# Two edits to a two-layer encoder kernel: the forgetting product over 128 rows, and the last down projection with positions on partitions

## The reference, cut to what matters

```python
def forgetting_attention(q, k, v, log_f):
    F = jnp.cumsum(log_f, axis=1)
    ...
        logits = jnp.einsum('bqhd,bshd->bhqs', q_blk, k) * (d ** -0.5)
        logits = logits + Fq[..., None] - Fk[:, :, None, :]
        logits = jnp.where(key_pos[None, :] <= qpos[:, None], logits, -jnp.inf)
    ...
    for l in range(DEPTH):
        h = h + hybrid_mixer(rmsnorm(h, norm1_g[l]), ...)
        h = h + (jax.nn.silu(gate) * up) @ w_down[l]     # gate, up: causal conv of h @ w_up
    return h * rsqrt(mean(h * h) + 1e-6) * final_g
```

## Time and profile before

| | before |
|---|---|
| median of 3 runs | 1531.95 us (1531.93 to 1532.08) |
| profiled execution | 1532.42 us |
| span of the profile | 1530.6 us |
| mean granted TensorE clock | 0.995 |
| TensorE (PE) busy | 1505.0 us, 98% of the span, 7184 products |
| VectorE (DVE) busy | 1015.4 us, 66% |
| ScalarE (ACT) busy | 705.4 us, 46% |
| GpSimd (POOL) busy | 49.3 us, 3% |
| HBM read, written | 136.13 MB, 2.10 MB |

### The profile page before, as it was taken

One profiled execution on the slowest core, in us unless ns is written; L12 is line 12 of the kernel. 1 busy time (PEld: TensorE's weight loads), 2 busy tenths in 40 slices (PEclk: granted clock), 3 DMA queues, 4 the chain that ended last, 5 costly groups with the idle time before them and its releaser, 6 DMA issues.

```text
span 1530.6 us, 20233 instructions
## 1 busy us (share of the span) xinstructions
PE 1505.0 (98%) x7184; PEld 1234.0 (81%) x7184; DVE 1015.4 (66%) x1818; ACT 705.4 (46%) x1214; POOL 49.3 (3%) x39
## 2 busy tenths in 40 slices
PE   7899999999999999999999999999999999999998
PEld 5688887788888888888878888778888888888886
DVE  5788775555587743777468887655557776257754
ACT  5766654433444422443376666433344443134444
POOL 0000000000200000000110000000020000000011
PEclk9999999999999999999999999999999999999998
DMA  6221212223232233232432222122323222332232
GB/s 228 69 75 64 77 55 80 73 84 117 84 109 93 86 94 113 96 96 69 126 123 83 70 70 70 56 82 70 110 69 124 97 96 83 97 109 96 84 91 73
DMA packets 43861, 139.27 MB, mean 91 GB/s; under 512 B 5508, under 2 KB 5636, under 8 KB 43528
## 3 DMA queue, kind: packets, MB, share of 16 engines
q1 hardware_dynamic: 43344, 137.45, 28.1%
q10 hardware_dynamic: 440, 0.80, 0.2%
HBM read 136.13 MB, written 2.10 MB: 90 GB/s over the span
## 4 chain that ended last, share of the span: by engine, by line
PE 92%; DVE 3%; ACT 2%; issue 1%; DMA 1%; SPq 0%; ACTq 0%; DVEq 0%
PE dense L574 28%; PE dense L576 28%; PE dense L575 28%; PE turned L619 2%; PE branch L633 2%; PE scores L605 1%; PE scores L606 1%; PE scores L609 1%; ACT tmp L927 1%; DMA h<-in_x 1%; DVE act L1154 0%; ACT whi L799 0%; PE dense L785 0%; DVE wlo L1074 0%; DVE act L1151 0%
## 5 line engine op out<-in xcount | busy, mean ns | idle before, releaser
L574 PE MATMUL dense<-hg,whi 128*128 128x512 f32 x1376 | 551.6, 401 | 13.6 <-DVE wlo L1088 7.2
L576 PE MATMUL dense<-hg,wlo 128*128 128x512 f32 x1376 | 539.1, 392 | 0.0
L575 PE MATMUL dense<-hg,whi 128*128 128x512 f32 x1376 | 538.5, 391 | 0.0
L799 ACT ACTIVATE whi<-raw 128x1024 fp32r<-128x1024 f32 (+3 forms) x275 | 266.6, 970 | 445.5 <-PE dense L576 444.6
L1074 DVE TENSOR_TENSOR wlo<-raw,whi 128x1024 fp32r<-128x1024 f32 (+3 forms) x275 | 306.7, 1115 | 168.9 <-ACT whi L799 165.9
L574 PEld LDWEIGHTS dense<-hg,whi 128*128 128x128 f32 x1376 | 260.7, 189 | 69.0 <-DVE wlo L1088 7.2
L576 PEld LDWEIGHTS dense<-hg,wlo 128*128 128x128 f32 x1376 | 259.8, 189 | 55.7
L575 PEld LDWEIGHTS dense<-hg,whi 128*128 128x128 f32 x1376 | 260.4, 189 | 50.5 <-issue 0.7
L574 PE MATMUL dense<-act,whi 128*128 128x512 f32 x608 | 238.9, 393 | 0.0
L576 PE MATMUL dense<-act,wlo 128*128 128x512 f32 x608 | 236.8, 389 | 0.0
L575 PE MATMUL dense<-act,whi 128*128 128x512 f32 x608 | 236.6, 389 | 0.0
(11 more groups left out here) (136 smaller groups left out, 1211.0 us busy)
## 6 DMA issues: line engine op xcount, KB each, us to landing
raw<-in_w_up SPq DMA_DIRECT2D x88, 512.0 KB, 3.5
raw<-in_w_gate SPq DMA_DIRECT2D x48, 512.0 KB, 3.4
raw<-in_w_in SPq DMA_DIRECT2D x35, 512.0 KB, 3.5
raw<-in_w_down SPq DMA_DIRECT2D x32, 384.0 KB, 3.0
raw<-in_w_down SPq DMA_DIRECT2D x32, 320.0 KB, 2.9
raw<-in_w_out SPq DMA_DIRECT2D x16, 512.0 KB, 3.6
raw<-in_w_br_a SPq DMA_DIRECT2D x8, 512.0 KB, 3.5
h<-in_x SPq DMA_DIRECT2D x8, 256.0 KB, 7.7
```

Source lines behind the costliest of these rows:

```text
L574: mm(out, a, xhi, start=start, stop=False)
L575: mm(out, a, xlo, start=False, stop=False)
L576: return mm(out, b, xhi, start=False, stop=stop)
L799: fn(whi[:, s, 0:cols], raw[:, r, 0:cols], ACT.Copy).then_inc(w_hi.sem, 1)
```

## The change

Forgetting term: `f_rows` is replaced by `fk`, one copy of the key rows for all 128 partitions, and `fq`, four copies of the query rows, one for each head, in which all rows outside the head's own 32 are zero (`own_rows`). The rows 32f + 4 to 32f + 31 hold zeros in both. A head's product now runs over all 128 rows, with four evacuations for the query side and one for the key side.

Last down projection: in layer 1's second half, `down_last` loads the activations (128 positions of a hidden chunk) into the array and streams 512 columns of weights. Its 10 units hold 2 hidden chunks by 512 output columns each; the first 5 make output columns 0 to 511, the last 5 columns 512 to 1023, with one bank of `dense` for each tile of 128 positions. h is transposed into the four attention banks after units 1 and 6. The last two units are mixed, so that position tiles 0 to 3 end one after another. Squares with a sum along the row replace the reduction over partitions; the final gain is a row that is loaded once and multiplied by GpSimd (first half) or VectorE (second half). The host puts the last down weights into a new order. Left out below: semaphore declarations, and the calls of `down_last` and `load_down_last` on the other engines.

```diff
--- before.py
+++ after.py
@@ -41,6 +41,8 @@
+LAST_GROUPS = HALVES[1] // 2
+LAST_UNITS = 2 * LAST_GROUPS
...
@@ -156,13 +158,14 @@
+    parts["own_rows"] = np.arange(P)[:, None] // 32 == np.arange(4)[None, :]
...
-        f_rows = sb("f_rows", [P, 2, S], F32R)
+        fq = sb("fq", [P, 4, S], F32R)
+        fk = sb("fk", [P, S], F32R)
...
+        y_sum = [[prob[t][:, :] for t in range(T)], [rel[:, t, :] for t in range(T)]]
+        y_gained = [out_st[:, t, 0:S] for t in range(T)]
+        gain_row, junk = tab[:, :, :].rearrange("p i s -> p (i s)"), tmp[0][:, :]
...
+        bank_r = [bank_s[0], bank_s[1], bank_t, bank_y]
...
+            def load_down_last(l):
+                for u in range(LAST_UNITS):
+                    f = DOWN0[1] + u
+                    s = f % RAW
+                    sp.wait_ge(w_lo.sem, w_lo.at(l, NMIX + f - RAW))
+                    sp.dma_start(raw[:, s, :], A["w_down_last"][u]).then_inc(raw_in[s], 16)
+                    if u == RAW:
+                        sp.wait_ge(used.sem, used.at(l, NMIX + DOWN0[1] - 1))
+                        sp.dma_start(gain_row, A["gain_row"]).then_inc(gain_row_in, 16)
...
-                sp.wait_ge(o_fin_a if i % 2 else o_fin_v, i // 2 + 1)
-                t, half = i // 2, i % 2
-                sp.dma_start(A["out"][0, t * P:(t + 1) * P, half * S:(half + 1) * S],
-                             out_st[:, t, half * S:(half + 1) * S]).then_inc(stored, 16)
+            for t in range(T):
+                for half in range(2):
+                    sp.wait_ge(o_fin_v if half else o_fin_a, t + 1)
+                    sp.dma_start(A["out"][0, t * P:(t + 1) * P, half * S:(half + 1) * S],
+                                 out_st[:, t, half * S:(half + 1) * S]).then_inc(stored, 16)
@@ -605,9 +632,8 @@
                 last = mm(b[:, 0:n], a, kk[:, 1, k0:k0 + n], start=False, stop=not forget)
                 if forget:
-                    f = 32 * (2 * (p - A_PAIRS - B_PAIRS) + s)
-                    last = mm(b[:, 0:n], f_rows[f:f + 4, 0, t * P:(t + 1) * P], f_rows[f:f + 4, 1, 0:n],
-                              start=False, stop=True)
+                    f = 2 * (p - A_PAIRS - B_PAIRS) + s
+                    last = mm(b[:, 0:n], fq[:, f, t * P:(t + 1) * P], fk[:, 0:n], start=False, stop=True)
                 last.then_inc(scores.sem, 1)
...
+            def turn_residual(t, dh):
+                if dh == 1:
+                    pe.wait_ge(fin_res, t + 1)
+                for c in range(4):
+                    last = nc.tensor.transpose(bank_r[t][:, c * P:(c + 1) * P],
+                                               h[:, 4 * dh + c, t * P:(t + 1) * P], ident[:, :])
+                last.then_inc(fin_tr, 1)
+            def down_last(l):
+                def tile(dh, g, t, last_g):
+                    s = (DOWN0[1] + dh * LAST_GROUPS + g) % SPL
+                    for c in range(2):
+                        ch = 2 * g + c
+                        if dh == 0 and t == 0:
+                            pe.wait_ge(glu_lo.sem, glu_lo.at(l, PAIR0[1] + ch))
+                        a, b = whi[:, s, c * S:(c + 1) * S], wlo[:, s, c * S:(c + 1) * S]
+                        a_hi, a_lo = act2[:, ch, 0, t * P:(t + 1) * P], act2[:, ch, 1, t * P:(t + 1) * P]
+                        mm(bank[t][:, :], a_hi, a, start=ch == 0, stop=False)
+                        mm(bank[t][:, :], a_hi, b, start=False, stop=False)
+                        last = mm(bank[t][:, :], a_lo, a, start=False, stop=last_g and c == 1)
+                    return last
+                for u in range(LAST_GROUPS):
+                    pe.wait_ge(w_lo.sem, w_lo.at(l, NMIX + DOWN0[1] + u))
+                    for t in range(T):
+                        if u == 0:
+                            pe.wait_ge(hp.sem, hp.at(l, 2 * FF - NBANK + t))
+                        last = tile(0, u, t, u == LAST_GROUPS - 1)
+                        if u == LAST_GROUPS - 1 and t < T - 1:
+                            last.then_inc(fin_mm, 1)
+                    last.then_inc(used.sem, 1)
+                    if u == 1:
+                        pe.wait_ge(h_mid.sem, h_mid.at(l, C - 1))
+                        for t in range(T):
+                            turn_residual(t, 0)
+                for u in range(LAST_GROUPS - 2):
+                    pe.wait_ge(w_lo.sem, w_lo.at(l, NMIX + DOWN0[1] + LAST_GROUPS + u))
+                    for t in range(T):
+                        if u == 0:
+                            pe.wait_ge(fin_sum, t + 1)
+                        last = tile(1, u, t, False)
+                    last.then_inc(used.sem, 1)
+                    if u == 1:
+                        for t in range(T):
+                            turn_residual(t, 1)
+                pe.wait_ge(w_lo.sem, w_lo.at(l, NMIX + DOWN0[1] + 2 * LAST_GROUPS - 2))
+                for t in range(2):
+                    tile(1, LAST_GROUPS - 2, t, False)
+                pe.wait_ge(w_lo.sem, w_lo.at(l, NMIX + DOWN0[1] + 2 * LAST_GROUPS - 1))
+                for t in range(T):
+                    if t >= 2:
+                        tile(1, LAST_GROUPS - 2, t, False)
+                    tile(1, LAST_GROUPS - 1, t, True).then_inc(fin_mm, 1)
...
                             up_pair(l, half, it * 2 + jj, jj, False)
-                    down(l, half)
-            pe.wait_ge(ssum_done.sem, ssum_done.at(L, -1))
-            for t in range(T):
-                last = mm(bank_t[:, t:t + 1], ssum[:, t * P:(t + 1) * P], mean[:, 0:1], start=True, stop=True)
-            last.then_inc(ms.sem, 1)
-            for i in range(2 * T):
-                t, half = i // 2, i % 2
-                if t == 0:
-                    pe.wait_ge(y_fin_a if half else y_fin_v, C // 2)
-                if i >= 4:
-                    pe.wait_ge(o_fin_a if i % 2 else o_fin_v, i // 2 - 1)
-                for c in range(4):
-                    last = nc.tensor.transpose(bank[i % 4][:, c * P:(c + 1) * P],
-                                               h[:, 4 * half + c, t * P:(t + 1) * P], ident[:, :])
-                last.then_inc(t_fin, 1)
+                    if (l, half) == (L - 1, 1):
+                        down_last(l)
+                    else:
+                        down(l, half)
...
@@ -974,6 +1042,30 @@
+            def down_last(l, last):
+                for u in range(LAST_UNITS):
+                    f = DOWN0[1] + u
+                    split_hi_ffn(l, f, f % RAW, SLOT)
+                    if u == 0:
+                        conv_tap2(l, 0, 1, PAIR0[1] + last)
+                    if u == 1:
+                        gated(l, 1, last, 1)
+                    if u == 2:
+                        fn(stat[:, 1, 0:1], eps, ACT.Sqrt)
+                    if u in (3, LAST_GROUPS + 2):
+                        dh = u // LAST_GROUPS
+                        if dh == 0:
+                            act.wait_ge(used.sem, used.at(l, NMIX + DOWN0[1] - 1))
+                        for t in range(T):
+                            act.wait_ge(fin_tr, dh * T + t + 1)
+                            fn(y_sum[dh][t], bank_r[t][:, :], ACT.Copy).then_inc(fin_res, 1)
+                    if u == LAST_GROUPS + 1:
+                        for t in range(T):
+                            act.wait_ge(fin_sum, t + 1)
+                            if t > 0:
+                                act.wait_ge(fin_sq, t)
+                            fn(junk, y_sum[0][t], ACT.Square, accum_out=mx[:, t:t + 1]).then_inc(fin_sq, 1)
...
-            def final_gain(c):
-                act.wait_ge(hg_lo.sem, hg_lo.at(L, c - C))
-                fn(h[:, c, :], h[:, c, :], ACT.Copy, scale=gain(2 * L, c)).then_inc(y_fin_a, 1)
-            for c in range(C // 2, C - 2):
-                final_gain(c)
-            act.wait_ge(ms.sem, ms.at(L, 0))
-            fn(stat[:, 0, :], bank_t[:, 0:T], ACT.Sqrt, bias=eps).then_inc(rms.sem, 1)
-            for c in range(C - 2, C):
-                final_gain(c)
-            act.wait_ge(rrms_fin, 1)
-            for i in range(1, 2 * T, 2):
-                act.wait_ge(t_fin, i + 1)
-                fn(out_st[:, i // 2, S:2 * S], bank[i % 4][:, :], ACT.Copy, scale=stat[:, 1, i // 2:i // 2 + 1]).then_inc(o_fin_a, 1)
+            def final_out(t):
+                act.wait_ge(fin_rec, t + 1)
+                fn(out_st[:, t, 0:S], y_gained[t], ACT.Copy, scale=stat[:, 1, t:t + 1]).then_inc(o_fin_a, 1)
+            act.wait_ge(fin_bias, 1)
+            act.wait_ge(fin_yg, T)
+            for t in range(T):
+                act.wait_ge(fin_sum, T + t + 1)
+                fn(junk, y_sum[1][t], ACT.Square, accum_out=nmx[:, t:t + 1]).then_inc(fin_sq, 1)
+                act.wait_ge(fin_sq, T + t + 1)
+                fn(stat[:, 0, t:t + 1], nmx[:, t:t + 1], ACT.Sqrt, scale=1.0 / D,
+                   bias=sums[:, t:t + 1]).then_inc(fin_root, 1)
+                if t > 0:
+                    final_out(t - 1)
+            final_out(T - 1)
...
                     else:
```

(97 more changed lines are left out.)

3 lines of the change are left out of this document (2 added, 1 removed).

## The result

| | before | changed |
|---|---|---|
| median | 1531.94 us (4 runs, 1531.2 to 1532.08) | 1519.74 us (4 runs, 1518.82 to 1520.09) |
| ratio, 95% interval | | 0.9923, 0.9910 to 0.9935 |
| profiled execution, span | 1532.42, 1530.6 us | 1519.53, 1517.7 us |

The account below looks back on a forecast made before the run. TensorE, holding 92% of the chain, was taken as the bound. Forgetting term 10.4 - 2.3 = 8.1 plus last down projection and tail 8.1 - 3.5 = 4.6 gave 12.7: 1531.95 - 12.7 = 1519.3 us, range 1516.4 to 1523.2.

Parts of the forecast that it names:

- both parts: Forgetting term with its added evacuations, 8.1 us gained; last down projection with the end of the kernel, 4.6 us gained.
- the tail: From last product to end of span: 6.9 us against 15.0, as 3.4 + 3.1 + 0.4; 8.1 gained.
- The forgetting product: 32 steps of the forgetting branch: full-row product in place of 4 rows saves 28 x 0.345 + 4 x 0.19 = 10.4 us.
- The two sub-terms: Each forgetting step: 0.19 to 0.20 us saved on the product, 0.15 on the three transposes behind it.
- the smaller saving before branch products: One of 8 forgetting steps per pair is followed by branch products and saves only 0.19 us.
- The page's rule: Rival for forgetting products: weight load exposed, 4.3 us saved in place of 10.4, 1525.4 us; chance 0.05.
- The wait at unit 15: Three more VectorE evacuations delay ScalarE's copy, so TensorE's transposes wait: 1.15 us a layer, 2.3 in all.
- The stage: Last down projection: products unchanged, 32 residual transposes at 0.11 us add 3.5 us on TensorE.
- The place that the prediction called tight: Last unit of the last down stage: weight split needs 2.45 us against 2.5 available; counted as 0 wait (0 to 0.5).
- The slower rival, the clock: Last down stage loses TensorE's upper clock level: 1573.7 us with all of the stage at the lower; chance 0.03.
- upper bound, 8.0 with four stores queued: End of the kernel: 8.0 us from last product to end if four stores within 1.2 us queue up.

Follow-up runs that it names:

- full_rows: Kernel before with only the forgetting product run over all 128 rows, no added evacuation, bias left wrong: 1520.86 us, ratio 0.9930.
- v_first: Changed kernel with each position tile's two stores swapped, VectorE's half before ScalarE's: 1519.05 us, ratio 0.9918.
- evac_alone: Kernel before with three more evacuations of the query rows at unit 15, result unused: 1534.03 us, ratio 1.0018.
- part1_alone: Kernel before with the whole forgetting-term change (fq, fk, five evacuations, full-row product), old last down projection and tail: 1522.94 us, ratio 0.9945.
- part2_alone: Changed kernel with the forgetting term of the kernel before, so only the last down stage and tail changed: 1528.18 us, ratio 0.9978.
- rows32: Kernel before with the forgetting product over 32 rows, 28 of them zeros, in place of 4: 1531.53 us, ratio 1.0000.
- rows64: Kernel before with the forgetting product over 64 rows, bias left wrong: 1532.12 us, ratio 1.0004.
- defer: Changed kernel with query rows evacuated once at unit 15 and four masked copies made at units 20 to 23: 1516.44 us, ratio 0.9902.
- plain_end: Changed kernel with the last two down units in plain order, all four tiles of unit 8, then of unit 9: 1520.05 us, ratio 0.9925.
- early_third: Changed kernel with v_first's store order and the third tile's output written before the wait for the last product: 1519.02 us, ratio 0.9915.
- best: Changed kernel with defer, v_first and the early third tile together: 1517.06 us, ratio 0.9904.
- best_two_queues: As best, with the last store of ScalarE's half issued from ScalarE's own queue: 1516.45 us, ratio 0.9901.

## Why the prediction was right, and where it was lucky

The savings and costs of both parts came where the prediction had placed them. One term of its sum was mis-sized, the tail, and the spread of the start hid a part of that.

**The forgetting product** (10.4 gained): 10.4 by product starts, 10.6 by the median of full_rows. The two sub-terms, 0.19 on the product and 0.15 behind it, and the smaller saving before branch products all stand in the rows. The page's rule that a load overlaps only when the row group differs (the Trainium skill, TensorE: Matmul & The Clock Gate, Part 3, The mechanism) did not hold here: 32 loads of 0.19 us vanish, 16 of them beside products that hold 0.12, and the measurement decides. The same section also says that a load goes ahead of running products when it targets "the background weight buffer", and these rows don't speak against that.

**The wait at unit 15** (2.3 lost): +1.13 and +1.15 in the changed kernel, 1.09 and 1.07 with the evacuations alone. The five evacuations took 3.6 us where two took 1.4, so VectorE was 2.2 late. The wait came where the prediction placed it, on ScalarE's copy. The earlier start of this kernel by 1.1 us moved all engines alike and changed nothing in it.

**The stage** (3.5 lost): 3.41. 32 transposes at 0.11 us, granted clock 1.00 from 1455 to the last product. The place that the prediction called tight, 2.45 against 2.5 us at the last unit, was tight: its first weight load waited for the low split,

```profile
PEld dense L802 <- DVE wlo L1170: 0.2, 1, 0.2
```

and the product behind it came 0.02 us late. The slower rival, the clock, never came near.

**The tail** (6.9): 7.9. This is the term that was mis-sized. Its first half was too long (3.4 to the last copy, measured 3.0, since the square took 0.63 and not 0.73, and neighbouring instructions on ScalarE overlap by 0.09 each), its second too short (3.5 from the copy to the end, measured 4.8). No table load stands in the tail: the root's is at 1458.6, in unit 2. The sum took the tail of before, where one store leaves behind the last output, and added one issue. But the third tile's VectorE half, ready at 1511.39, stood in SyncE's queue behind ScalarE's half, ready at 1512.2; four stores then left between 1512.25 and 1513.91, the last one issued 1.07 us after the last output and not 0.4, and 0.35 of that is the unexplained pause. v_first takes 0.7 of the whole back. The other tenths are the last landing (2.7 against 2.3) and the wait in the closing step (0.5 against 0.2). The prediction had this case as its upper bound, 8.0 with four stores queued, and did not put it in the sum.

**The start.** The prediction's terms with their measured sizes give 10.4 - 2.3 - 3.4 + 7.1 = 11.8, and the medians 12.2. The spans give 12.9, because the profiled execution of before was 1.1 us later than that of the changed kernel 86 us in. The other profiles, against before at the same product: full_rows -0.74, evac_alone -1.00, part1_alone -1.39, part2_alone -0.96, rows32 -1.10, rows64 -0.61, defer -1.18, v_first -2.09, plain_end -1.13, early_third +0.11, best -0.41, best_two_queues -2.32. Kernels that share the start's code to the letter lie up to 2.4 us apart, so this is a spread from execution to execution. So the closeness is partly luck: the tail was off by 1.0 us, and the medians, which gained 0.4 more than the terms, show a miss of 0.4 only; on the two spans the start would have hidden all of it. The forecast also put the median 0.5 us below the profiled execution, as it was before; in the changed kernel it is 0.2 above.

## What to carry to other kernels

Price a product by what it holds in the chain and by what the next one holds: one product on a part of the rows, put between full ones, cost up to 0.34 us more than a full-row product, which holds 0.12, and filling the other rows with zeros was cheaper. Work added to an engine with idle time is free only as far as there is slack behind it before the bounding engine waits: 2.2 us in one piece at unit 15 cost 1.1, and pieces of 0.48 one a unit at units 20 to 23 cost nothing. Compare stages by the start of the same instruction, since two spans here differed by up to 2.4 us before the first edited line.

## What the runs showed that I had not expected

Products over 32 and 64 rows hold as much as over 4 (0.31 us at 256 keys). An evacuation with two scalars per partition took 0.80 us where the one with one scalar (line 1225 before, line 1326 in the changed kernel) took 0.75, and the mask alone, from SBUF, 0.48. From the last output to the end of the span stay 4.1 us with two last stores ready together, on one queue or two, against 3.1 before. On one queue (best) that is 1.04 to issue both, 0.35 of it a pause, 2.3 to land and 0.7 to close, against 0.47, 2.3 and 0.4 before. With two queues it is 0.4, 3.0 and 0.7: why the landing takes the longer, and what the pause and the longer close are, stays open.
